# Interleaving a delta rule with the projections and attention heads of its own block

## What is computed

```python
h = rmsnorm(x, ln1[l])
proj = h @ w_in[l]
qkv_a, z_a, b_a, a_a, q_b, k_b, v_b = jnp.split(proj, IN_SPLITS, axis=-1)
y_a = gated_deltanet(qkv_a, z_a, b_a, a_a, conv_qkv[l], a_log[l], dt_bias[l], gdn_norm[l])
y_b = dilated_attention(heads_b(q_b), heads_b(k_b), heads_b(v_b), slopes)
x = x + jnp.concatenate([y_a, y_b], axis=-1) @ w_out[l]
...
# gated_deltanet: q, k = l2norm(silu(conv(...))), 4 heads of 128; then per head, in 4 tiles of 128 tokens here:
a = strict lower part of (k_beta k^T) * decay        # triangular_solve((I + a), [v*beta, k*beta*exp(g)])
v_new = u - w @ state;  o = q_dec @ state + a_qk @ v_new;  state = state * decay_last + k_dec^T @ v_new
y = o * rsqrt(mean(o*o) + eps) * norm_gain * silu(z)
```

## Time and profile before

| | us |
|---|---|
| three runs: median (lowest, highest) | 3092.21 (3087.30, 3094.47) |
| the profiled execution: its time, its span | 3093.37, 3091.6 |
| TensorE busy, share of the span | 2767.5, 90% |
| VectorE busy | 1301.1, 42% |
| ScalarE busy | 984.6, 32% |
| GpSimd busy | 327.5, 11% |
| mean granted clock of TensorE | 0.915 |

### The profile page before, as it was taken

The page is one execution under the profiler, slowest core; times in us unless marked ns, Lnnn a source line. Parts: engine busy times, 40 slices in busy tenths (PEclk is TensorE's granted clock), DMA queues, the critical chain, the costliest instruction groups (busy, mean ns, idle before and its releaser), DMA issues.

```text
span 3091.6 us, 35367 instructions
## 1 busy us (share of the span) xinstructions
PE 2767.5 (90%) x13904; PEld 1585.0 (51%) x13904; DVE 1301.1 (42%) x2560; ACT 984.6 (32%) x1831; POOL 327.5 (11%) x181
## 2 busy tenths in 40 slices
PE   6999998799999995988969999986999677799998
PEld 3875554333333322865433333323876367687886
DVE  2585523334444444655242332225514653343242
ACT  4224422234444335234122222213233223332222
POOL 0110001001111101200000000000220041122221
PEclk9998989799999997988989999997995578899999
DMA  6226623599999995200149999995321000122321
GB/s 233 66 71 228 225 78 123 187 323 350 350 364 358 352 364 195 82 28 1 41 142 387 386 386 386 387 386 184 91 87 34 8 1 1 62 83 95 95 89 48
DMA packets 303260, 568.52 MB, mean 184 GB/s; under 512 B 12656, under 2 KB 55792, under 8 KB 302968
## 3 DMA queue, kind: packets, MB, share of 16 engines
q1 hardware_dynamic: 294480, 545.33, 49.8%
q0 software_dynamic: 3840, 12.59, 1.8%
q10 hardware_dynamic: 4776, 8.35, 0.8%
HBM read 551.54 MB, written 14.68 MB: 183 GB/s over the span
## 4 chain that ended last, share of the span: by engine, by line
PE 70%; DVE 7%; DMA 6%; ACT 3%; issue 1%; POOL 0%; ACTq 0%; DVEq 0%; SPq 0%
PE PS L887 19%; PE PS L893 6%; PE PS L836 5%; PE PS L989 4%; PE PS L990 4%; PE PS L988 4%; PE PS L941 2%; PE PS L1002 2%; PE PS L1003 2%; PE PS L1004 2%; PE PS L654 2%; DMA WIDE<-in_w_gate_dram 2%; PE PS L978 2%; DMA RING<-in_w_gate_dram 1%; PE PS L1021 1%
## 5 line engine op out<-in xcount | busy, mean ns | idle before, releaser
L887 PE MATMUL PS<-RING,RF 128*64 128x512 f32 x1448 | 353.8, 614 | 13.6 <-DMA RING<-in_w_gate_dram 3.9
L887 PE MATMUL PS<-WIDE,RF 128*64 128x512 f32 x1408 | 331.4, 600 | 9.9 <-DMA WIDE<-in_w_gate_dram 3.6
L2407 POOL TENSOR_TENSOR WHL<-RING,WHL 128x1024 fp32r<-128x1024 f32 x54 | 145.6, 2696 | 1270.6 <-ACT WHL L1197 1270.6
L887 PEld LDWEIGHTS PS<-RING,RF 128*64 128x64 f32 x1448 | 92.7, 138 | 223.1 <-issue 200.0
L989 PE MATMUL PS<-RR,WHL 128*128 128x512 f32 x512 | 203.7, 398 | 0.0
L990 PE MATMUL PS<-RR,WHL 128*128 128x512 f32 x512 | 203.1, 397 | 0.0
L988 PE MATMUL PS<-RR,WHL 128*128 128x512 f32 x512 | 202.2, 395 | 0.8 <-DVE RR L2170 0.8
L887 PEld LDWEIGHTS PS<-WIDE,RF 128*64 128x64 f32 x1408 | 92.7, 136 | 204.7 <-issue 182.3
L1428 ACT ACTIVATE RF<-PS,MODS,MSC 128x128 f32<-128x128 f32 x192 | 77.4, 438 | 302.5 <-PE PS L941 155.9
L1197 ACT ACTIVATE WHL<-RING 128x1024 fp32r<-128x1024 f32 (+1 forms) x109 | 113.7, 1047 | 188.3 <-PE PS L1004 113.3
L1666 DVE TENSOR_TENSOR WHL<-RING,WHL 128x1024 fp32r<-128x1024 f32 (+1 forms) x55 | 67.9, 1234 | 229.5 <-ACT WHL L1197 229.5
(11 more groups left out here) (384 smaller groups left out, 5037.6 us busy)
## 6 DMA issues: line engine op xcount, KB each, us to landing
RING<-in_w_gate_dram SPq DMA_DIRECT2D x83, 1024.0 KB
WIDE<-in_w_down_dram SPq DMA_DIRECT2D x74, 1024.0 KB, 9.4
RING<-in_w_up_dram SPq DMA_DIRECT2D x70, 1024.0 KB
WIDE<-in_w_up_dram SPq DMA_DIRECT2D x57, 1024.0 KB, 11.9
RING<-in_w_down_dram SPq DMA_DIRECT2D x51, 1024.0 KB
RING<-in_ada_w_dram SPq DMA_DIRECT2D x48, 1024.0 KB
WIDE<-in_w_gate_dram SPq DMA_DIRECT2D x45, 1024.0 KB, 10.9
RING<-in_w_in_dram SPq DMA_DIRECT2D x27, 1024.0 KB
```

Of the source, the lines that this page charges most:

```text
L887: ins = e.matmul(a[r:r + 64, :], xs[:, j, 0:64], w[:, i, :], start=j < 2, stop=j > 5)
L2407: e.tensor_tensor(lo, load_buffer(loads[st["load"]])[:, js, cs], h.bitcast(F32), ALU.subtract).then_inc(pool, G(("lo", st["i"])))
```

## The change

A list, second_plan, now gives one order of small pieces for all engines, and each engine's function `between` walks through it. Its first part has the 16 projection steps left after the bg step, in the order qb, kb, vb, z (z is moved behind vb). Between them stand the norms' squares, sums and scalings, the turns, the decays and GpSimd's products. Its second part has 37 steps, k = 0 to 36. Step k holds the attention's loop turn k (the last transpose of a head pair one turn later than before) and then pieces of the delta rule: a head's products and masks in k = 0 to 3, its first transpose one step later; from k = 4 one round and head of cm, and from k = 5 its du and dt one step after its cm; nw in k = 26 to 29; the chunk loop from k = 30. What is left of the chunk loop follows step 36, and the eight pairs of mix are made in two groups, 4 to 7 in step 36 and 0 to 3 at the end.

To have room for both at once, buffers move: the attention's work lies in WIDE, the delta rule's copies WS in the part of X that was the ring's fourth buffer. So the w_in2 loads use a ring of three, and the first w_out2 load, which goes to the fourth, waits for the solve's last product. The first three mix steps' halves are made in step 36 behind the pairs 4 to 7. The attention and projections take banks from a ring of four (flow), the delta rule from the other four (rule). The causal mask of a head moves from VectorE (L2234) to GpSimd, SiLU of z goes ahead of the attention, and both parts of hconst are loaded early.

```diff
@@ weight_steps: order of the loads, ring slots, look-ahead @@
-    second = len(loads)
     for c0 in (0, 512, 1024):
         add(w_in2[:, c0:c0 + 512], 8, 512, "f")
-    add(w_in2[:, 1536:2048], 8, 512, "k")
     add(w_in2[:, 2048:2056], 8, 8, "f")
     for c0 in (2056, 2568):
         add(w_in2[:, c0:c0 + 512], 8, 512, "f")
     add(w_in2[:, 3080:3592], 8, 512, "k")
+    add(w_in2[:, 1536:2048], 8, 512, "k")
+    third, mix = len(loads), len(steps)
     for half in (0, 512):
         add(w_out2[:, half:half + 512], 8, 512, "k")
...
-    for ld in loads[second:]:
+    for ld in loads[third:]:
         ld["slots"] = (0, 1, 2, 3)
+    for st in steps[mix:mix + LOOK + 1]:
+        st["behind"] = True
...
+    next(ld for ld in loads[third:] if ld["slot"] == NRING)["scratch"] = True
...
+        if used == mix:
+            ahead.append(steps[mix:mix + LOOK + 1])
+            done = mix + LOOK + 1
         while done < len(steps) and done <= used + LOOK:
+            if used < mix <= done:
+                break
@@ second_plan, new @@
+def second_plan():
+
+
+    plan = []
+    later = [("col", n, c) for n in ("qb", "kb") for c in range(4)] + [("tok", n, k) for n in ("vb", "z") for k in (0, 2, 4, 6)]
+    units = (4, 5, 6, 7, 0, 1, 2, 3)
+    for k, piece in enumerate(later):
+        if 0 < k <= 8:
+            plan.append(("sum", k - 1, units[k - 1]))
+        if k < 8:
+            plan.append(("square", k, units[k], units[k - 2]))
+        plan.append(piece)
+        if 0 < k <= 8:
+            plan.append(("unit", k - 1, units[k - 1]))
+        if k == 3:
+            plan.append(("scalars",))
+        if 1 <= k <= 4:
+            plan.append(("turn", k - 1, 8))
+        if 5 <= k <= 8:
+            plan += [("turn", k - 5, 4), ("values", k - 5)]
+        if k == 9:
+            plan.append(("eg",))
+        if 10 <= k <= 13:
+            plan += [("decay", k - 10), ("keys", k - 10)]
+        if k == 14:
+            plan.append(("kdc",))
+        if k >= 14:
+            plan += [("kdec", 2 * (k - 14)), ("kdec", 2 * (k - 14) + 1)]
+    plan.append(("zsilu",))
+
+    wy = [(s, h) for s in range(1, 7) for h in range(4)]
+    chunks = [("vnew", 0), ("out", 0), ("vnew", 1), ("gate", 0), ("out", 1), ("flip", 0), ("vnew", 2), ("gate", 1),
+              ("out", 2), ("flip", 1), ("vnew", 3), ("gate", 2), ("out", 3), ("flip", 2), ("gate", 3), ("flip", 3)]
+    starts = {("vnew", 0): 30, ("out", 0): 31, ("vnew", 1): 32, ("gate", 0): 32, ("out", 1): 33, ("flip", 0): 34}
+    for k in range(37):
+        if k < 36:
+            plan.append(("attend", k))
+        if k < 4:
+            plan.append(("head", k))
+        if 1 <= k <= 4:
+            plan += [("first", k - 1), ("mask", 1, k - 1)]
+        if 0 <= k - 5 < 24:
+            plan.append(("onward", *wy[k - 5]))
+        if 0 <= k - 4 < 24:
+            n, h = wy[k - 4]
+            plan.append(("cm", n, h))
+            if n < 6:
+                plan.append(("mask", n + 1, h))
+        if 26 <= k < 30:
+            plan.append(("nw", k - 26))
+        while chunks and k >= starts.get(chunks[0], 35 if chunks[0][0] != "flip" else 36):
+            plan.append(chunks.pop(0))
+            if chunks and chunks[0] not in starts:
+                break
+        if k == 36:
+            plan += [("y2", 4), ("y2", 5), ("y2", 6), ("y2", 7), ("early",)]
+    return plan + chunks + [("y2", j) for j in range(4)]
+
@@ buffers (a part) @@
-        YH = rf(5120, 4, 128)
-        UU, TT_ = rf(2048, 4, 512), rf(4096, 4, 512)
-        AT, AQ = rf(6144, 4, 512), rf(8192, 4, 512)
-        WS = [rf(10240, 512), rf(10752, 512), ar(12288, 512), ar(12800, 512)]
-        CMS = [rf(11264, 512), TM0, TM1, rf(11776, 512)]
+        UU, TT_, AT, AQ = rf(0, 4, 512), rf(2048, 4, 512), rf(4096, 4, 512), rf(6144, 4, 512)
+        WS = [XS[:, 512 * i:512 * i + 512] for i in range(4)]
+        CMS = [CON[:, C_ROPE:C_ROPE + 512], TM0, TM1, ROW[:, R_QK:R_QK + 512]]
+        AZ, RESET = TM0[0:4, :], TM1[0:4, :]
@@ sync: the first load of w_out2 into the scratch @@
+                if "scratch" in ld:
+                    e.wait_ge(pe, P["du", 6, 3])
@@ tensor: the plan on its two rings of banks @@
+            def between():
+                flow, rule = Ring([(i,) for i in range(4)], freed), Ring([(i,) for i in range(4, 8)], freed)
+                for what, *k in plan2:
+                    if what == "col":
+                        columns([(A, tuple(k))], ring=flow)
+                    elif what == "tok":
+                        tokens(flow, (k[0],), A, 8, k[1], lambda j: HTH2[:, j, :], lambda j: HTL2[:, j, :])
+                    elif what == "attend":
+                        attend2(flow, *k)
+                    elif what == "sum":
+                        i, f = k
+                        o = bank(rule, ("l2", f), (V, ("l2", f)))
+                        e.wait_ge(act, A["sq2", f])
+                        e.matmul(o, ONE, SQ[i % 2], start=True, stop=True).then_inc(pe, P(("l2", f)))
...
+                    elif what == "head":
+                        h, = k
+                        for name, f, free in (("kk", 4 + h, "kkd"), ("bb", 0, "at"), ("kq", h, "aq")):
+                            o = bank(rule, (name, h), (V, (free, h)))
+                            if name == "bb":
+                                ins = e.matmul(o, HSEL[:, 128 * h:128 * h + 128], BR, start=True, stop=True)
+                            else:
+                                for z in tiles4:
+                                    ins = e.matmul(o[:, z], C[:, 4 + h, z], C[:, f, z], start=True, stop=True)
+                            ins.then_inc(pe, P((name, h)))
...
+                    elif what == "cm":
+                        n, h = k
+                        o = bank(rule, ("cm", n, h), (A, ("ws", n, h)))
+                        e.wait_ge(pool, G["cm", n, h])
+                        if n == 1:
...
+                            e.wait_ge(dve, V["tu", n - 1, h])
...
+                    elif what == "onward":
+                        n, h = k
+                        o = bank(rule, ("du", n, h), (V, ("tu", n, h)))
@@ scalar: the first three mix steps' halves @@
+                    if "behind" in st:
+                        e.wait_ge(dve, V["y2", 7])
@@ vector, in head: the causal mask comes from GpSimd @@
+                        e.wait_ge(dve, V.n)
+                        e.scalar_tensor_tensor(u3, u3, -1.0, idb, ALU.mult, ALU.add).then_inc(dve, V(("u0", h)))
+                        e.tensor_copy(DL[:, h, :], CMS[h].rearrange("p (t i) -> p t i", i=128)[:, :, 127]).then_inc(dve, V())
+                        e.wait_ge(pe, P["kq", h])
+                        e.wait_ge(pool, G["causal", h])
```

More of the change, by code:

```diff
@@ new lines, in tokens @@
+            def tokens(ring, name, on, k, n, hi, lo_):
+                st, h, lo = weights()
+                for t in range(4):
+                    if n == 0:
+                        bank(ring, (*name, t), (on, (*name, t)))
+                    o, z = held(*name, t), tiles4[t]
+                    for i in range(2):
+                        j = n + i
+                        e.matmul(o, hi(j)[:, z], h[:, i, :], start=j == 0, stop=False)
+                        e.matmul(o, hi(j)[:, z], lo[:, i, :], start=False, stop=False)
+                        ins = e.matmul(o, lo_(j)[:, z], h[:, i, :], start=False, stop=j == k - 1)
+                    names = [(*name, t)] if n == k - 2 else []
+                    if t == 3:
+                        ins.then_inc(pe, P(("w", st["i"]), *names))
+                    elif names:
+                        ins.then_inc(pe, P(*names))
@@ L1161, in tensor @@
                 ins.then_inc(pe, P(*([("w", st["i"]), ("bg", 1)] if i else [("bg", 0)])))
-            columns([(A, ("qb", c)) for c in range(4)])
-            columns([(A, ("kb", c)) for c in range(4)])
-            tokens(("vb",), A, 8, HTH2, HTL2)
-            second_attention()
-            delta_rule()
+            between()
             e.wait_ge(dve, V["y2", 3])
             for half in range(2):
-                tokens(("mix2", half), V, 8, YH2, YL2)
+                for n in range(0, 8, 2):
+                    tokens(every, ("mix2", half), V, 8, n, lambda j: YH2[j], lambda j: YL2[j])
             turn_tiles(HN3, "2c", lambda j: ("x3T", j), lambda j: (V, ("x3T", j)))
@@ L1178, in tensor @@
                     for half in range(2):
-                        tokens(("down2", part, half), V, nf, GH, GL)
+                        for n in range(0, nf, 2):
+                            tokens(every, ("down2", part, half), V, nf, n, lambda j: GH[:, j, :], lambda j: GL[:, j, :])
         def scalar(e):
```

774 lines of the change are left out of this document (394 added, 380 removed).

## The result

| | median us | lowest to highest | ratio to before (95%) |
|---|---|---|---|
| before, same chip | 3093.34 | 3087.30 to 3095.05 | |
| changed kernel | 2988.43 | 2986.10 to 2993.54 | 0.9666 (0.9648 to 0.9685) |

The change gains 105 us. The prediction was 2994 us with a range of 2960 to 3040, so it was right, 6 us too slow. The profiled execution took 2986.1 us with a span of 2984.3; before it was 3093.37 and 3091.6. The mean clock rose from 0.915 to 0.943.

A forecast was written before the change was run, and what follows sets the result against it. Attention and delta rule chains run one after the other, neither filling the other engines; interleaved, 22 + 36 + 117 + 47 = 222 us replace 320.1, a gain of 98, giving 2994 us against the median, range 2960 to 3040.

The forecast's parts named there:

- projections: Last block's projections with norms, turns and decays between them: the norms hide, the stage grows by 22 us, bounds 17 and 45.
- steps 0 to 4: Start of the second part, the heads beside the first attention items, led by VectorE: 36 us, bounds 27 and 45.
- steps 5 to 28: Second part's loop with the solve between attention items: 24 steps of 4.75 us plus 3, 117 us, bounds 103 and 140.
- the rest to mix: Steps 29 to 36 and the old tail up to mix's first matmul: 47 us, bounds 37 and 57.
- behind mix's start: Mix and the feed-forward after the last block: all keep their time, mix beginning at the low clock as before.
- The two later waits of 1.2 and 1.7 us: Projections: the next two root and remainder steps inherit the scan's lateness through ScalarE's queue, 1.2 and 1.7 us.
- The start term: Opening of the second part: ScalarE's four SiLUs, 4.4 us, then the first bias transfer, 2.9 us; 7.3 us on the path.
- The collisions: Heads in the second part's first steps: GpSimd's masking lengthens VectorE passes with two SBUF inputs, 1.4 us a step.
- so not TensorE but this loop binds: Solve steps: the loop over the scores' bank, bias pass and solve's updates takes 4.76 us against TensorE's 4.26.
- the rival of 3084: Clock stays low through the loop of steps 5 to 28: 8.5 us a step, 90 us more, 3084 us; chance 6%.
- steps 32 to 35: Chunk loop late in the second part: two v_new of 1.8 us, two sets of o and increment with copy; 12 us.
- The table loads that go were beside VectorE's passes and give nothing: Tail before mix: the table loads the change removes lay beside VectorE's passes, so their removal gains nothing.

The follow-up runs named there:

- z_first: Changed kernel with VectorE's bias pass ahead of the solve's updates; additionally z projected before the values, SiLUs and first two bias transfers under the values' projection: 2977.02 us.
- mask_on_vector: Changed kernel with only the heads' causal mask moved back from GpSimd to VectorE: 2986.98 us, ratio 0.9657.
- gate_ahead: Changed kernel plus bias pass before updates, pairs 4 to 6 in the loop, unread matmuls before mix, chunk 1's gate ahead of chunk 2's v_new: 2968.84 us.

## Why the prediction was right, and where it wasn't

| term | predicted | measured |
|---|---|---|
| projections | +22 | +18.2 |
| steps 0 to 4 | 36 | 34.1 |
| steps 5 to 28 | 117 | 109.2 |
| the rest to mix | 47 | 55.2 |
| sum, in place of 320.1 | 222 | 216.7 |
| behind mix's start | 0 | -3.9 |

That the sum is off by only 5 us is in part luck: three terms were 13.5 us too long together, the fourth 8.2 too short.

**Projections.** The norms hide. What TensorE's matmuls waited for ahead of the eight sums (L1127; us, times):

```profile
  ACT CON L1607: 1.9, 1
```

It waited 1.9 us for the first square (I had said about 2) and not again; the sums follow every 6.9 us. The two later waits of 1.2 and 1.7 us did not come. They rested on the scan's 3.25 us, and that was no duration of the scan. GpSimd's remainder had started 0.4 us before it; in the changed kernel, where the scan is first, it takes 1.21, and GpSimd's 3.27. First VectorE's row of after, then GpSimd's of before and after:

```profile
2245.04 1.21 DVE L2487 TENSOR_TENSOR_SCAN VECY<-TM,VECY 4x512 f32<-4x512 f32 x1
```

```profile
2267.07 2.54 POOL L2407 TENSOR_TENSOR WHL<-RING,WHL 128x1024 fp32r<-128x1024 f32 x1 [21.00 <-ACT WHL L1197]
```

```profile
2245.19 3.27 POOL L2526 TENSOR_TENSOR WHL<-RING,WHL 128x1024 fp32r<-128x1024 f32 x1 [17.85 <-ACT WHL L1292]
```

**Steps 0 to 4.** The sum was right, its parts weren't, and that is luck. The start term, 7.3 us for SiLUs and bias transfer, was not on the path: z_first took it away and S stayed. What fills these 6 us is head 0 itself, which I had counted behind it as overlapping. The collisions cost 3.1 us and not 5.6. The low clock was there: in the last head VectorE waited 1.36 and 1.38 us for products of 2.0 us that take 1.1 at the full clock. By the Trainium skill, page "SBUF — State Buffer", section "SBUF: two separate sides", a VectorE operation with two SBUF inputs and a GpSimd operation that reads SBUF exclude each other for the whole instruction; the trace and mask_on_vector agree (1.32 and 1.09 us beside GpSimd, 0.69 without), how much is lost depends on how the two meet: 0.44 us in one pass, 0.95 in the next.

**Steps 5 to 28.** The period was met, 4.76 predicted and 4.71 measured, and TensorE's waits are for the bias pass behind the updates, as forecast. But "so not TensorE but this loop binds" was true for one step in four only. I had half a microsecond of waiting in each step and 4.26 us of TensorE's own work; it was 0.2 us of waiting in the mean and 4.49 of work (89.71/20). The two errors cancel, and the close number is luck. Undoing the loop left TensorE's own 4.43. What made the term too long is the number of such steps: the last four have no dt, and the nw lie inside them; with 20 x 4.71 and 15 for the four it is 109. The clock held at 1.00; the rival of 3084 fell, and the experiments with the attention alone show that it had been near: there it does fall. The first block's attention, which I held against this rival, has other shapes: 96 of its 170 matmuls there are 128*64 128x128, and none moves only 64 columns.

**The rest.** 8 us too short, and most of it in steps 32 to 35: 17.7 us (2496.33 to 2514.07) where I had 12. TensorE waited 1.89 us for item 31's bias and 2.25 for the last scaling, and behind these waits v_new of tiles 1 and 2 ran partly at the low clock, 3.2 and 2.9 us where I had 1.8. Step 36 took 10.3 us for 9.5: the remainder beside GpSimd took 2.54 us where the earlier trace rows had 1.23. The end took 18.8 for 17: behind its wait of 7.3 us TensorE made o of tile 3 at the low clock, 3.7 us in place of 2.0.

**Table loads.** The step "the table loads that go were beside VectorE's passes and give nothing" nearly held inside the tail: in the last gate of before the loads held back the root by 0.4 us and the last product by 0.3. It failed behind the tail, for the load that the tail's last root makes needless.

## What to carry to other kernels

When two independent chains of one block are woven into one order, count the gain by stage and look whether TensorE holds its clock in each chain alone: over half of the second part's gain here is that, by the estimate above. Two part changes that both carry a third one can't be added up, even where the sum comes out right. An order of pieces for an in-order machine should read each piece's input before the partner's long update is queued on the same engine; here one such swap on VectorE was worth 12 us. A wait that disappears from a chain of two other engines came back here one instruction later (7.3 us became 9.3 elsewhere). Taking work off the chain gained 2.4 us of S.

## What the runs showed of the hardware that I had not expected

- A TensorE that was 93 to 94% busy stayed at the low clock for 51 and for 94 us; dense matmuls raised it within 3 us. Waits of about 1 us sometimes went ahead of a fall and sometimes not.
- A pass of VectorE can be stretched by GpSimd even when it has almost nothing to do: one over 4 columns took 1.51 us (2.01 in gate_ahead) in place of 0.17, a scan of 4 partitions 3.25 in place of 1.21.
- A table load of 1.28 us in front of a waiting TensorE cost 3.3 us, since the clock fell with it.
- Three matmuls that nobody reads, in TensorE's waits, made the next stage start at the full clock and gained 2 us.
